# Combining expert outputs in PSUM with row tiles, at 32 slots an item

## The reference

```
xn = RMSNorm(x);  proj = xn @ w_in  ->  [B_a | C_a | H_a | GLU_a | GLU_b | gates]
y_a = (B_a * conv3(C_a * H_a)) @ w_out_a
y_b = swish(LN(conv31(GLU_a * sigmoid(GLU_b)) + b)) @ w_out_b + b_out_b
x   = x + (sigmoid(gA) * y_a + sigmoid(gB) * y_b) @ w_o
x   = x + HierMoE(RMSNorm(x))     # top-1 of 4 groups, then top-2 of its 8 experts
y   = RMSNorm(x)
```

## Time and profile before

| | |
|---|---|
| median of 3 timed runs | 918.84 us (918.76 to 918.95) |
| profiled execution, own time | 922.34 us |
| its span, first to last instruction | 920.6 us |
| mean granted clock of TensorE | 0.965 |
| PE busy / PEld / DVE / ACT / POOL | 90% / 68% / 62% / 33% / 29% |
| DMA: bytes, mean rate | 250.00 MB, 272 GB/s |

### The profile page before, as it was taken

The page is one execution under the profiler, slowest core; times in us unless marked ns, Lnnn a source line. Parts: engine busy times, 40 slices in busy tenths (PEclk is TensorE's granted clock), DMA queues, the critical chain, the costliest instruction groups (busy, mean ns, idle before and its releaser), DMA issues.

```text
span 920.6 us, 22534 instructions
## 1 busy us (share of the span) xinstructions
PE 826.8 (90%) x8395; PEld 623.0 (68%) x8396; DVE 568.6 (62%) x1516; ACT 307.8 (33%) x536; POOL 270.7 (29%) x136
## 2 busy tenths in 40 slices
PE   2999999999999999379799979788999999989993
PEld 2999999999999998346355535454655555555561
DVE  3056987999942342636366766546656765656756
ACT  4432875464358331821122221212121222211112
POOL 3745899795767782400000000000000000000000
PEclk9999999999999999579799999999999999999997
DMA  5733333325424422929899999999999999999701
GB/s 209 232 113 126 129 117 117 134 94 189 136 92 137 137 75 63 424 93 391 318 395 422 422 421 422 422 421 422 421 422 421 422 422 422 422 422 421 324 0 68
DMA packets 53144, 250.00 MB, mean 272 GB/s; under 512 B 6570, under 2 KB 6570, under 8 KB 28532
## 3 DMA queue, kind: packets, MB, share of 16 engines
q1 hardware_dynamic: 49184, 244.86, 67.3%
q10 hardware_dynamic: 3923, 4.67, 1.7%
HBM read 246.76 MB, written 2.75 MB: 271 GB/s over the span
## 4 chain that ended last, share of the span: by engine, by line
PE 66%; DMA 15%; DVE 12%; issue 3%; ACT 2%; ACTq 0%; SPq 0%; DVEq 0%
PE bank L1307 23%; PE bank L1433 15%; DMA ring<-in_exp_w_up 14%; PE bank L1476 9%; DVE bank L945 7%; PE bank L1395 7%; PE bank L1426 5%; PE bank L1305 4%; PE bank L1465 2%; DMA stage<-in_norm_g 1%; DVE ua L1007 1%; PE bank L1368 1%; ACT cvb L704 1%; PE bank L1404 0%; ACT w_hi L627 0%
## 5 line engine op out<-in xcount | busy, mean ns | idle before, releaser
L506 POOL TENSOR_TENSOR w_lo<-raw,w_hi 128x2048 fp32r<-128x2048 f32 x40 | 184.8, 4622 | 77.8 <-ACT w_hi L627 77.7
L1433 PE MATMUL bank<-ring,cvb 128*32 128x256 f32 x2816 | 169.0, 394 | 41.1 <-DMA ring<-in_exp_w_up 20.5
L1433 PEld LDWEIGHTS bank<-ring,cvb 128*32 128x32 f32 x2816 | 92.3, 113 | 130.6 <-issue 83.2
L1307 PE MATMUL bank<-x_hi,w_hi 128*128 128x384 f32 x448 | 150.8, 337 | 0.3 <-DVE ua L964 0.2
L1307 PE MATMUL bank<-x_hi,w_lo 128*128 128x384 f32 x448 | 149.7, 334 | 0.0
L1307 PE MATMUL bank<-x_lo,w_hi 128*128 128x384 f32 x448 | 149.7, 334 | 0.0
L945 DVE SCALAR_TENSOR_TENSOR bank<-ub,vec,bank 128x256 f32<-128x256 f32 (+1 forms) x416 | 137.1, 411 | 0.0
L1476 PE MATMUL bank<-ring,cvb 128*64 128x512 f32 x560 | 127.9, 598 | 0.0
L1194 DVE SCALAR_TENSOR_TENSOR cvb<-bank,slot_coef,cvb 64x256 f32<-64x256 f32 x70 | 31.2, 487 | 127.6 <-ACT cvb L814 127.6
L627 ACT ACTIVATE w_hi<-raw 128x2048 fp32r<-128x2048 f32 x40 | 76.6, 1917 | 84.5 <-PE bank L1307 76.1
L823 ACT ACTIVATE y_hi<-bank 64x512 fp32r<-64x512 f32 x70 | 41.4, 591 | 175.8 <-PE bank L1476 174.9
(11 more groups left out here) (219 smaller groups left out, 1081.9 us busy)
## 6 DMA issues: line engine op xcount, KB each, us to landing
ring<-in_exp_w_gate SPq DMA_DIRECT2D x64, 1024.0 KB, 18.8
ring<-in_exp_w_up SPq DMA_DIRECT2D x64, 1024.0 KB, 20.8
ring<-in_exp_w_down SPq DMA_DIRECT2D x64, 1024.0 KB, 20.1
raw<-in_w_in SPq DMA_DIRECT2D x28, 1024.0 KB, 5.2
raw<-in_w_out_a SPq DMA_DIRECT2D x4, 1024.0 KB, 5.0
raw<-in_w_out_b SPq DMA_DIRECT2D x4, 1024.0 KB, 5.0
raw<-in_w_o SPq DMA_DIRECT2D x4, 1024.0 KB, 5.0
out<-n_tok ACTq DMA_DIRECT2D x3, 512.0 KB, 2.7
```

The lines of the kernel that those rows point to most:

```text
L506: pool.tensor_tensor(w_lo[u % NW][:, :, :], raw[u % NW][:, :, :], w_hi[u % NW][:, :, :].bitcast(F32), ALU.subtract).then_inc(lo_ready, 1)
L1307: ins = pe.matmul(b, wp[:, k % UK, cols], xp[:, k, :], start=start, stop=stop)
L1433: last = pe.matmul(gate_and_up(second)[q * TQ:(q + 1) * TQ, :], xe[:, k, second * TQ:(second + 1) * TQ], wide(slots[q // 2])[:, k, q % 2 * ...
```

## The change

- T is 32: an item holds 32 slots, and there are 44 items. The quarters and the numbering of combines are gone; ScalarE and VectorE run a single loop over all items, TensorE still loops over experts and reads two numbers at each.
- x is summed in PSUM. Banks 2 to 7 hold the 384x1024 residual during the expert stage. They are set to `x_tok` by six matmuls with the identity (`seed`), four of them after the router's logits. Nothing adds on VectorE; the final Square and scaling read the banks.
- Each item's rows are combined at once, by 24 matmuls in three turns. The y of an item is 32 slots by 1024 columns, stored as four blocks of 32 partitions with 256 columns each; each block is a row tile of 32 partitions, and the four tiles of a turn write to four different banks.
- The hidden products, their transpose and y share bank 1, so gate and up of the next item wait for `y_ready`. `down` is 32 matmuls in four column tiles.
- The gather is placed anew: four blocks after `down`, two after gate and up, one after each of the first two turns of combine.
- The rows of vectors are 13 DMAs instead of nine, a single row being split in 16 pieces; they are issued before ScalarE's table load, and the sample rows of x have a semaphore of their own.

The diff, cut to this:

```diff
+    T = 32
+    TILES = P // T
     QE = DE // 2
...
+    for a, b in zip(range(aux("pos"), len(AUX)), (0, 1, 2, 3, 2, 3)):
+        AUX_BANK[a] = b
...
-        HT = bank[2][:, 0:HK * T]
-        Y = bank[3]
...
+        HT = bank[1][:, 0:HK * T]
+        Y = bank[1][:, 0:QE]
+        GU = bank[1][:, 0:QE]
+
+        def total(t, h):
+
+            return bank[2 + 2 * t + h]
...
+            taps_b = conv_b_w.rearrange("l k d -> (l k) d")
+            rows = [(V_CB, taps_b[0:16]), (V_CB + 16, taps_b[16:KB_TAPS]),
+                    (V_N1, norm1_g), (V_GATE, gate_b.rearrange("l (a d) -> (l a) d", d=D)),
+                    (V_CA, conv_a_w.rearrange("l k d -> (l k) d")), (V_CBB, conv_b_b), (V_LNG, ln_b_g), (V_LNB, ln_b_b), (V_BO, b_out_b), (V_N2, norm2_g)]
+            for r, src in rows:
+                if src.shape[0] > 3:
+                    act.dma_start(stage[r:r + src.shape[0], 0, :], src).then_inc(vec_in, 16)
+                else:
+                    for a in range(src.shape[0]):
+                        act.dma_start(stage[r + a:r + a + 1, 0, :].rearrange("a (c n) -> a c n", c=16),
+                                      src[a:a + 1].rearrange("a (c n) -> a c n", c=16)).then_inc(vec_in, 16)
+
...
-                    act.activation(sig[:, second * QE:(second + 1) * QE], gate_and_up(second)[0:T, :], ACT.Silu)\
-                       .then_inc(sig_ready, 1)
+                act.activation(sig, GU[0:2 * T, :], ACT.Silu).then_inc(sig_ready, 1)
                 act.wait_ge(hid_turned, i + 1)
                 act.activation(hidT.rearrange("p k t -> p (k t)"), HT, ACT.Copy).then_inc(hidT_ready, 1)
 
-                if c is not None:
-                    act.wait_ge(combined, c * NT + NT)
+                act.wait_ge(combined, i * NT + (NT + 1))
                 act.wait_ge(down_done, i + 1)
+                act.activation(y_hi[:, :], Y, ACT.Copy).then_inc(y_hi_ready, 1)
...
+            def pick_tokens(pick_n):
+
+                dve.tensor_tensor(chosen, iota[:, :].unsqueeze(1).to_broadcast([P, 2 * NT, T]),
+                                  slot_rem.rearrange("p c i -> p (c i)").unsqueeze(2).to_broadcast([P, 2 * NT, T]),
+                                  ALU.is_equal).then_inc(chosen_ready, 1)
+                dve.wait_ge(chosen_ready, pick_n + 1)
+                dve.tensor_tensor(pick, chosen[:, 0:NT, :], chosen[:, NT:2 * NT, :], ALU.add).then_inc(picked, 1)
...
+            def next_coefficients():
+
+                flat = spread_rows.rearrange("p c n -> p (c n)")
+                dve.scalar_tensor_tensor(at_slot.rearrange("p c n -> p (c n)"), flat[:, 0:2 * N],
+                                         own_slot[:, 0:1], flat[:, 2 * N:4 * N], ALU.is_equal, ALU.mult,
+                                         accum_out=slot_coef[:, 0:1]).then_inc(slot_coef_ready, 1)
...
+
+
+                dve.wait_ge(slot_coef_ready, i + 1)
...
+                dve.wait_ge(combined, i * NT + (NT + 1))
+                dve.scalar_tensor_tensor(back_to[:, :], spread_rows[:, 1, :], own_slot[:, 0:1], at_slot[:, 0, :],
                                          ALU.is_equal, ALU.add).then_inc(back_ready, 1)
...
+                dve.wait_ge(y_hi_ready, i + 1)
+                dve.tensor_tensor(y_lo[:, :], Y, y_hi[:, :].bitcast(F32), ALU.subtract).then_inc(y_ready, 1)
+
+            with dve.Fori(0, items) as i:
+                item(i)
...
+            wait_aux_read(pe, aux("logit", NT - 1))
+            for t in range(1, NT):
+                for h in range(2):
+                    seed(t, h)
...
             items = pe.value_load(table[0:1, 2 * NE:2 * NE + 1], min_val=NE, max_val=MAX_ITEMS)
-            last_back = pe.value_load(table[0:1, 3 * NE + 1:3 * NE + 2], min_val=NE // 2, max_val=MAX_ITEMS)
             spread(2)
             spread(3)
...
-            def combine(t, c):
-
-
-                pe.wait_ge(tile_added, c * NT + (NT, NT - 1, NT + 1)[t])
-                for h, b in enumerate(back(t)):
-                    for part, y in enumerate((y_hi, y_lo)):
-                        last = pe.matmul(b[:, :], back_to[:, t * P:(t + 1) * P], y[:, h * HALF:(h + 1) * HALF],
-                                         start=(part == 0), stop=(part == 1))
+
+            LATE = KB // 2
+            pe.wait_ge(picked, 2)
+            pe.wait_ge(xe_ready, 1)
+            gather(range(LATE))
+
+            def combine(turn, last_item=False):
+
+                for y in (y_hi, y_lo):
+                    for q in range(TILES):
+                        t = (turn + q % 2) % NT
+                        rows, cols = slice(q * T, (q + 1) * T), slice(q % 2 * QE, (q % 2 + 1) * QE)
+                        last = pe.matmul(total(t, q // 2)[:, cols], back_to[rows, t * P:(t + 1) * P], y[rows, :],
+                                         start=False, stop=last_item and y is y_lo and turn > q % 2)
                 last.then_inc(combined, 1)
...
-            def item(i, slots, filled, c, second_slots):
+            def item(i, slots, filled):
...
                 pe.wait_ge(xe_ready, i + 1)
+                pe.wait_ge(y_ready, i + 2)
...
+                    for k in range(part * KB // 2, (part + 1) * KB // 2):
+                        for q in range(TILES):
+                            last = pe.matmul(GU[q * T:(q + 1) * T, :], xe[:, k, :],
+                                             wide(slots[q // 2])[:, k, q % 2 * QE:(q % 2 + 1) * QE],
+                                             start=(k == 0), stop=(k == KB - 1))
+                    last.then_inc(done, 1)
+
+                gather([LATE, LATE + 1])
+                pe.wait_ge(back_ready, i + 1)
+                pe.wait_ge(combined, i * NT + 1)
+                combine(0)
+                gather([LATE + 2])
+                pe.wait_ge(combined, i * NT + 2)
+                combine(1)
                 pe.wait_ge(hid_ready, i + 1)
-                gather([early])
...
+                turned = HT.rearrange("p (h c t) -> p h c t", h=2, c=HK // 2)
+                cols = hid.rearrange("t (q c) -> t c q", c=HK // 2)
+                for c2 in range(HK // 2):
+                    last = pe.transpose(turned[:, :, c2, :], cols[:, c2, :], ident[0:2 * T, 0:2 * T])
                 last.then_inc(hid_turned, 1)
-                gather(range(early + 1, KB - 2))
-                if c is not None:
-                    combine(2, c)
-                gather(range(KB - 2, KB))
+                pe.wait_ge(combined, i * NT + 3)
+                combine(2)
                 pe.wait_ge(hidT_ready, i + 1)
...
+                        for q in range(TILES):
+                            last = pe.matmul(Y[q * T:(q + 1) * T, :], hidT[:, k, :],
+                                             deep(slots[2])[:, k, q * QE:(q + 1) * QE],
...
+                pe.wait_ge(picked, i + 3)
+                pe.wait_ge(xe_ready, i + 2)
+                gather(range(LATE))
+
+            for a in ("spread", 2), ("spread", 3):
+                wait_aux_read(pe, aux(*a))
+            seed(0, 0)
+            seed(0, 1).then_inc(combined, 1)
             with pe.Fori(0, NE // 2) as pair:
-                for par in range(2):
-                    e = pair * 2 + par
+                for side in range(2):
+                    e = pair * 2 + side
                     n = pe.value_load(table[0:1, bass.ds(e, 1)], min_val=1, max_val=N // T)
                     first = pe.value_load(table[0:1, bass.ds(e + NE, 1)], min_val=0, max_val=MAX_ITEMS - 1)
-                    slots = [3 * par + c for c in range(3)]
+                    slots = [3 * side + c for c in range(3)]
...
+                    with pe.Fori(0, n) as j:
+                        item(first + j, slots, filled)
...
+            for turn in range(NT):
+                pe.wait_ge(combined, items * NT + (turn + 1))
+                combine(turn, True)
```

More of the change, by code:

```diff
@@ L841, in _ @@
-            load_root_table(3)
-            for i in range(NT):
-                act.wait_ge(tile_added, last_back * NT + (NT + i + 1))
-                if i:
-                    act.wait_ge(ssq_ready, 2 * NT + i)
-                act.activation(junk, x_tok[:, i, :], ACT.Square, accum_out=small[:, 16 + i:17 + i]).then_inc(ssq_ready, 1)
+                act.activation(y_hi[:, :], Y, ACT.Copy).then_inc(y_hi_ready, 1)
+            with act.Fori(0, items) as i:
+                item(i)
+            load_root_table(3)
@@ L848, in _ @@
+            act.wait_ge(combined, items * NT + (NT + 1))
+            for i in range(NT):
+                for h in range(2):
+                    if i or h:
+                        act.wait_ge(ssq_ready, 2 * NT + 2 * i + h)
+                    at_col = (16, 42)[h] + i
+                    act.activation(junk[:, 0:HALF], total(i, h)[:, :], ACT.Square, accum_out=small[:, at_col:at_col + 1])\
+                       .then_inc(ssq_ready, 1)
                 act.wait_ge(root_in, 4 + i)
@@ L1370, in _, with seed @@
                 end_aux(last)
+            def seed(t, h):
```

(21 more changed lines are left out.)

251 lines of the change are left out of this document (61 added, 190 removed).

## The result

The kernel after takes 949.76 us (949.38 to 951.51, 4 runs) against 918.89 us (918.76 to 919.89, 4 runs): a ratio of 1.0324, 95% interval 1.0307 to 1.034. It is 30.9 us slower; 939 was forecast. The profiled execution took 949.38 us, its span is 947.6 us, 27.0 more than the span of before, whose profiled execution was itself 3.5 us above its median.

What follows compares the result with a forecast made beforehand. DMA was taken to bound the kernel from 520 us, TensorE from 654.16 us. Terms +22.3 + 1 − 3 = +20.3 us on a 920.6 us span gave 940.9; with the median 1.8 below the span, 939 us, range 929 to 951.

Steps and rivals of the forecast that it cites:

- Experts 17 to 31, the main term: Last 15 experts, TensorE the limit: 25 items of 32 slots take 269.2 us against 246.9, +22.3 us.
- Changes inside a pair: Expert changes: table reads and branch behind the gather make 11.1 us gate to gate inside a pair, 11.7 between pairs.
- Row tiles: Combine: four row tiles run and load beside each other, 0.216 us a round, 1.28 us for six rounds.
- changes of tile shape: Each item on TensorE: six turns between steps of other tile shapes at about 0.1 us each, 0.6 us.
- rival of loads in a row: Combine: the four loads of a round cannot overlap, a round takes 0.43 us, 968 us in all; chance 0.18.
- Trainium skill's 3.07 times: Combine: row tiles gain 3.07 times, not four; six rounds take 1.67 us instead of 1.28, 949 us in all.
- The gather: Each item on TensorE: 21 ns a pair, 0.19 us a block; the four blocks behind down are hidden.
- Ahead of 654 us: Everything before the last stretch: +1 us at 654 us, bounds −4 and +3.
- little arrives at the end: First weight unit up to 5 us earlier, −4.5 taken, but nearly all lost where expert 4 waits for expert 3's transfer.
- The end: From the last down to the first Square: 4.0 us instead of 7.1; with Squares and scaling −3, bounds −2 and −3.5.
- Hidden boundaries: Expert changes: the queue takes the branch before the gather, so the sequencer's work stays hidden, 922 us; chance 0.14.
- The other side: Last stretch: 15 ns gather pairs, free tile-shape changes, hidden boundaries; an item takes 9.3 us, 909 us in all; chance 0.18.

Runs made afterwards that it cites:

- experiment 2: Kernel after with the counts read ahead as in experiment 1, and VectorE subtracting y_lo before the next coefficients: 924.37 us, ratio 1.005 to before.
- experiment 1: Kernel after without TensorE's two table reads at a change of expert, the next count being loaded in mid gate and up: 929.41 us, ratio 1.0104 to before.
- experiment 3: Kernel after with two more table reads at each expert on TensorE, values not used: 992.30 us, ratio 1.0771 to before.
- experiment 4: Kernel after with the four gather blocks moved from behind down to the head of the next item, ahead of gate and up: 933.20 us, ratio 1.0154 to before.
- experiment 6: Kernel before with only the change's 13 vector DMAs and the sample rows' own semaphore: 916.28 us, ratio 0.9957 to before.

## Why the prediction was right, and where it was not

- **Experts 17 to 31, the main term** (+22.3 forecast, +35.1 measured). Inside an expert 9.8 was forecast and 10.03 measured: +2.3 in all. The bound was named wrongly: VectorE "has finished" by then, I wrote; it had not, its coefficients stood ahead of `y_lo` (experiment 2). Changes inside a pair, 11.1 forecast and 11.11 measured; between pairs 11.7 and 11.50, −1.4. That these are the sequencer's reads behind the gather is shown by experiments 1, 3 and 4. `down` 8.6 and 8.41. Waits for weights 3 and 3.25, but that is luck: they were forecast around experts 22 to 26, where after has none, and came at expert 17. What was missing is a term, the half clock: seven gate and up at +1.69, **+11.8 us**, the largest error. I had costed the idleness at changes at its own length and nothing else, though the earlier trace rows and the clock at 0.99 showed what TensorE had to lose.
- **Row tiles.** Four do start together, 0.22 us a round, as computed from the column tiles of the earlier trace rows. (The untiled combine there takes 0.48 ns a column, so the tiled one takes 1.75 times that, and not twice; the sum does not use it.) The changes of tile shape cost less than my 0.6: three turns of 0.44 are 1.32, and each of the three blocks of gather ahead of a turn or of the transposes takes 0.31 or 0.32 instead of 0.24, 0.2 in all. The rival of loads in a row is refuted: a load of 128 columns takes 0.18 us in the mean and the four of a round 0.19 together, hidden behind the matmuls. The estimate from the Trainium skill's 3.07 times ("TensorE: Matmul & The Clock Gate", measured speedup vs the span model) was 949, which is the measured time, but not for its reason. The trace does not agree with the term: six rounds take 1.32 us, and not 1.67.
- **The gather.** A block starts 0.24 us after the one before it (907.69, 907.93), 27 ns a pair, not 21, where 64 columns took 29: halving the columns that move gives almost nothing. The four blocks behind `down` were hidden, as costed.
- **Ahead of 654 us** +1 forecast, −3.6 measured in spans. The execution of before that was profiled is 3.5 us above its median, though; from experiment 6 (648.19, in a kernel whose median is 3.5 us lower) I estimate that a median execution starts expert 17 near 651.7, which leaves about −1. The step "little arrives at the end" failed even so: the first product came 2.8 us earlier (19.32 against 22.09; I had sized the gain of the first unit at 4.5), and experiment 6 keeps the gain. In after the reads took most of it back: without them expert 17 starts at 644.86 (experiment 1) instead of 650.55.
- **The end** −3 forecast, −4.5 measured: the six rounds ran at a granted clock of 1.00, 1.7 us (934.17 to 935.88), not at half pace (2.6) as the twelve matmuls of the earlier trace rows, whose clock was 0.50. That is 0.9 of the 1.5 us; the rest is open.
- **The range.** That 949.8 lies under 951 is in part luck. The range was made of the gather, the changes of shape and what is ahead of 654 us, and the 11.8 us of clock that filled it were not among them.
- **The rivals.** Hidden boundaries (922) is what experiments 1 and 4 build on purpose (929 and 933). The other side needed both that and shorter gathers, and the transfers, I think, would have caught it, as they did in experiment 1.

## What to carry to other kernels

Halving a tile halves the work that scales with it, and everything else is paid more often (here 25 times instead of 18): the combine, the drains, the handover of y, and 0.65 to 0.8 us for every number that a sequencer must read before it can issue (two more in experiment 3, three in the earlier trace rows). Ask of each boundary not how long the engine idles but whether the idleness also drops its clock: here changes that took 1.1 to 1.5 us longer cost another 0.8 on average in clock. Reads of loop counts belong in the middle of a long run of matmuls, one step ahead; that was worth 20 us in one kernel and about 7 in the other. Once TensorE is faster, look at the transfers again: here waits for weights kept nearly half of what the reads and the clock gave back (experiment 1).

## What the runs showed of the hardware

- fp32 matmuls with 32- or 64-column tiles take 0.84 ns a moving column with two or four tiles side by side; row tiles of 32 partitions do the same (four of 256 columns in 0.22 us).
- A load of 128 columns of bf16 weights and its matmul start every 27 ns with 32 columns moving (after, 907.69 to 907.93) and every 29 ns with 64 (before).
- The granted clock fell (to 0.68 in the mean of a gate and up) behind 7 of 14 changes of expert at which TensorE had idled for 1.7 to 2.1 us. With 3.0 to 3.4 us of idleness (experiment 3) it fell behind all 15 changes, and with at most 1 us at a time (experiments 1 and 4) behind none; all this from expert 17 on. Behind 3.0 us of waiting for weights in the middle of gate and up it fell in two of three cases (experiment 1, clocks of 0.57 and 0.53 in the first 2 us).
